# Splitting slabs 36 to 39 of the input projection and moving the recurrence's phase products to VectorE

## The reference

```python
h = _rmsnorm(x, p['norm_mix_w'])
a_v, a_g, b_u, c_z, c_xbc, c_dt = jnp.split(h @ p['w_in'], IN_SPLITS, axis=-1)
ya, conv_a_buf = _conformer_conv(a_v, a_g, ...)
yb, s5_re, s5_im = _s5(b_u, s5_re, s5_im, ...)
yc, conv_c_buf, ssd_state = _mamba2(c_z, c_xbc, c_dt, ...)
x = x + jnp.concatenate([ya, yb, yc], axis=-1) @ p['w_out']
```

## Time and profile before

| | us |
|---|---|
| median of 3 runs | 1803.45 (1802.83 to 1803.63) |
| the profiled execution | 1805.04 |
| its span, first to last instruction | 1803.3 |
| PE busy in the span | 1784.9 (99%) |
| DVE busy | 1139.3 (63%) |
| ACT busy | 739.2 (41%) |
| POOL busy | 258.9 (14%) |

### The profile page before, as it was taken

How to read it: one execution, slowest core, us unless ns; L and a number is a source line. 1 busy time by engine, 2 the same in 40 slices (tenths; PEclk the granted TensorE clock), 3 DMA queues, 4 the chain that set the end, 5 groups by cost and what they waited for, 6 DMA issues and landing times.

```text
span 1803.3 us, 32857 instructions
## 1 busy us (share of the span) xinstructions
PE 1784.9 (99%) x12594; PEld 1640.2 (91%) x12594; DVE 1139.3 (63%) x1976; ACT 739.2 (41%) x1111; POOL 258.9 (14%) x273
## 2 busy tenths in 40 slices
PE   8999999999999999999999999999999999999998
PEld 7877898777779999866999999999999999999998
DVE  6999888888775564443456556665655566546444
ACT  3100575444453343342245344444433345444444
POOL 1024200133421310000132000000000000003200
PEclk9999999999999999999999999999999999999999
DMA  8333544556667585487555555555555556554552
GB/s 255 106 117 106 198 140 138 176 182 208 196 209 240 164 303 164 153 327 265 154 164 164 164 163 163 163 163 164 164 166 165 165 148 185 166 163 160 167 163 99
DMA packets 158390, 316.49 MB, mean 176 GB/s; under 512 B 16986, under 2 KB 39531, under 8 KB 153492
## 3 DMA queue, kind: packets, MB, share of 16 engines
q1 hardware_dynamic: 153525, 307.73, 54.5%
q10 hardware_dynamic: 4776, 7.56, 1.4%
HBM read 300.78 MB, written 14.89 MB: 175 GB/s over the span
## 4 chain that ended last, share of the span: by engine, by line
PE 93%; DVE 4%; DMA 2%; ACT 1%; issue 0%; ACTq 0%; SPq 0%; DVEq 0%
PE bank L909 22%; PE bank L911 21%; PE bank L910 21%; PE bank L872 20%; PE bank L1467 2%; PE bank L1479 1%; DVE xc L2638 1%; DMA kv<-in_cache_mem_v 1%; DMA xtok<-in_x_prompt 1%; PE bank L1489 1%; PE bank L1278 0%; DMA raw<-in_w_out 0%; DVE raw_lo L2665 0%; PE bank L1097 0%; PE bank L958 0%; PE bank L1312 0%
## 5 line engine op out<-in xcount | busy, mean ns | idle before, releaser
L909 PE MATMUL bank<-hhi,whi 128*128 128x288 f32 x2128 | 631.9, 297 | 0.9 <-DVE wlo L2918 0.9
L910 PE MATMUL bank<-hlo,whi 128*128 128x288 f32 x2128 | 628.5, 295 | 0.0
L911 PE MATMUL bank<-hhi,wlo 128*128 128x288 f32 x2128 | 626.3, 294 | 0.0
L2918 DVE TENSOR_TENSOR wlo<-raw,whi 128x1024 fp32r<-128x1024 f32 (+1 forms) x270 | 329.7, 1222 | 377.7 <-ACT whi L1950 377.1
L1950 ACT ACTIVATE whi<-raw 128x1024 fp32r<-128x1024 f32 (+1 forms) x270 | 283.2, 1049 | 509.8 <-PE bank L911 501.9
L911 PEld LDWEIGHTS bank<-hhi,wlo 128*128 128x128 f32 x2128 | 401.6, 189 | 0.0
L909 PEld LDWEIGHTS bank<-hhi,whi 128*128 128x128 f32 x2128 | 399.3, 188 | 2.3 <-DVE wlo L2918 1.9
L910 PEld LDWEIGHTS bank<-hlo,whi 128*128 128x128 f32 x2128 | 400.2, 188 | 0.1
L872 PE MATMUL bank<-hT,raw 128*128 128x288 f32 x640 | 160.1, 409 | 0.0
L872 PEld LDWEIGHTS bank<-hT,raw 128*128 128x128 f32 x640 | 120.0, 190 | 35.0 <-issue 3.1
L1877 ACT ACTIVATE khi<-raw 128x1024 fp32r<-128x1024 f32 x66 | 69.9, 1059 | 109.5 <-PE bank L872 106.4
(11 more groups left out here) (551 smaller groups left out, 2744.4 us busy)
## 6 DMA issues: line engine op xcount, KB each, us to landing
raw<-in_ffn_w_down SPq DMA_DIRECT2D x86, 512.0 KB, 3.8
raw<-in_ffn_w_gate SPq DMA_DIRECT2D x80, 512.0 KB, 3.7
raw<-in_ffn_w_up SPq DMA_DIRECT2D x80, 512.0 KB, 3.7
raw<-in_w_in SPq DMA_DIRECT2D x64, 512.0 KB, 3.7
raw<-in_xa_wk SPq DMA_DIRECT2D x32, 512.0 KB, 3.9
raw<-in_xa_wv SPq DMA_DIRECT2D x32, 512.0 KB, 4.2
raw<-in_w_out SPq DMA_DIRECT2D x32, 512.0 KB, 3.8
raw<-in_xa_wq SPq DMA_DIRECT2D x32, 512.0 KB, 4.0
```

The costliest lines, as they stand in the source:

```text
L909: pe.matmul(out, lhsT=wh[:, wo:wo + P], rhs=xh, start=first, stop=False)
L910: pe.matmul(out, lhsT=wh[:, wo:wo + P], rhs=xl, start=False, stop=False)
L911: return pe.matmul(out, lhsT=wl[:, wo:wo + P], rhs=xh, start=False, stop=last)
L2918: tt(wlo[:, s % 2, wsl], raw[:, s % 4, wsl], whi[:, s % 2, wsl].bitcast(F32), ALU.subtract)\
```

## The change

1. `SPLIT_AT` becomes 36: slabs 36 to 39 are split too. Group 4 is then half plain (slabs 32 to 35, row tiles 0 to 7) and half split (slabs 36 to 39, row tiles 8 to 15).
2. ACT rounds the activations of tiles 8 to 15 right after `in_evac(3)`, ahead of the first taps, and those of tiles 0 to 7 between the splits; `XHI_AT` gives each tile's place in the new order. The functions `first_tap`, `taps_c` and `gelu` only move in the text, and the four first taps with them.
3. The phase products leave POOL and become `s5_products` on DVE, of the step before, between `tAB` and `gri` of a step.
4. `s5_turn_back(j - 1)` moves from the end of step j to the place between `gri` and the scan.
5. DVE's `in_split` of slabs 36 to 41 is placed inside steps 14 and 15 and behind them.
6. `s5_out` of the last pair comes after slab 40 instead of 39.

```diff
-    "pool_setup": (("bsel", 2), ("s5_prod", 2 * SJ), ("s5_fin", 2), ("conf_sum", 2)),
+    "pool_setup": (("bsel", 2), ("s5_fin", 2), ("conf_sum", 2)),
...
-        SPLIT_AT = 40
+        SPLIT_AT = 36
+        XHI_AT = [k - 8 if k >= 8 else k + 8 for k in range(16)]
+        S5_OUT = (22, 25, 27, 30, 32, 35, 37, 40)
...
-            for j in range(SJ):
-                pool.wait_ge(*at("s5_scanned", j + 1))
-                g_ = gri[:, j % 2, :, :]
-                if j >= 1:
-                    pool.wait_ge(*at("s5_h", 2 * j))
-                pool.tensor_tensor(hAB[:, 0, :, :], g_, tabC[:, j, :].unsqueeze(1).to_broadcast([P, 2, NP]),
-                                   ALU.mult).then_inc(S("s5_prod"), 1)
-                pool.tensor_tensor(hAB[:, 1, :, :], g_, tabS[:, j, :].unsqueeze(1).to_broadcast([P, 2, NP]),
-                                   ALU.mult).then_inc(S("s5_prod"), 1)
...
-                                    pe.wait_ge(*at("x_hi", k + 1))
+                                    pe.wait_ge(*at("x_hi", XHI_AT[k] + 1))
...
-                    if x == S5_IN[pair] + 5:
+                    if x == S5_OUT[pair]:
                         s5_out(pair)
...
-                    wait_used_A(sc_, SPLIT_AT - 8 + k // 2)
+                    wait_used_A(sc_, (24 if k >= 8 else 32) + k // 2)
...
+            x_high(range(8, KT))
+
+            def first_tap(dst, dst_s, src, src_s, w, b, name):
...
+            for t in range(4):
+                sc_.wait_ge(*at("u_done", 2 * t + 2))
+                first_tap(va[:, t, 0:NP], vsplit(va[:, t, NP:T], NB), up[:, t, 0:NP], up_sample(t)[:, :, 0:NL],
+                          col(C_CAW + t), col(C_CAB + t), "tap_a")
...
-            x_high(range(12))
-            in_split(SPLIT_AT)
-            x_high(range(12, 14))
+            in_split(36)
+            x_high(range(4))
+            in_split(37)
+            x_high(range(4, 8))
+            in_split(38)
+            in_split(39)
+            in_split(40)
             in_evac(4)
-            in_split(SPLIT_AT + 1)
-            x_high(range(14, KT))
+            in_split(41)
...
-            for x in range(SPLIT_AT, NA):
+            for x in range(40, NA):
...
+            def s5_products(j):
+
+                v.wait_ge(*at("s5_scanned", j + 1))
+                g_ = gri[:, j % 2, :, :]
+                if j >= 1:
+                    v.wait_ge(*at("s5_h", 2 * j))
+                for i, tab in enumerate((tabC, tabS)):
+                    tt(hAB[:, i, :, :], g_, tab[:, j, :].unsqueeze(1).to_broadcast([P, 2, NP]), ALU.mult)\
+                        .then_inc(S("s5_prod"), 1)
...
             for j in range(SJ):
+                if j == 15:
+                    in_split(38)
                 v.wait_ge(*at("s5_in", j // 2 + 1))
...
+                if j == 14:
+                    in_split(36)
+                if j >= 1:
+                    s5_products(j - 1)
                 v.wait_ge(*at("s5_turned", 2 * j + 2))
                 g_ = gri[:, j % 2, :, :]
                 if j >= 2:
                     v.wait_ge(*at("s5_prod", 2 * (j - 1)))
                 me.step(tt(g_[:, 0, :], tAB[:, 0, 0, :], tAB[:, 1, 1, :], ALU.add))
                 me.step(tt(g_[:, 1, :], tAB[:, 0, 1, :], tAB[:, 1, 0, :], ALU.subtract))
-                me.sync()
+                if j == 15:
+                    in_split(39)
+                gri_done = me.n
+                if j >= 1:
+                    s5_turn_back(j - 1)
+                me.reach(gri_done)
                 mag = sc[:, 14, j:j + 1].to_broadcast([P, NP])
...
                 if 2 <= j < 10:
                     x_low((6 + j,))
-                if j >= 1:
-                    s5_turn_back(j - 1)
+                if j == 14:
+                    in_split(37)
+                if j == 15:
+                    in_split(40)
...
+            s5_products(SJ - 1)
+            in_split(41)
             s5_turn_back(SJ - 1)
...
-            in_split(SPLIT_AT)
-            in_split(SPLIT_AT + 1)
```

More of the change, by code:

```diff
@@ L1768, in _, with x_high, in_split @@
             in_evac(3)
+            def x_high(tiles):
+                for k in tiles:
+                    wait_used_A(sc_, (24 if k >= 8 else 32) + k // 2)
+                    sc_.wait_ge(*at("x_lo", k + 1))
+                    a(xhi[:, k, :], hT[:, k, :], ACT.Copy).then_inc(S("x_hi"), 1)
+            def in_split(x):
+                wait_raw(sc_, x // 4, x % 4)
+                if x >= SPLIT_AT + 2:
+                    wait_used_A(sc_, x - 2)
+                if x == 48:
+                    sc_.wait_ge(*at("s5_prod", 2 * SJ))
+                    sc_.wait_ge(*at("s5_turned", 2 * SJ))
+                a(ihi_slot(x), raw[:, x % 4, :], ACT.Copy).then_inc(S("kw_hi"), 1)
+            x_high(range(8, KT))
             def first_tap(dst, dst_s, src, src_s, w, b, name):
@@ L1790, in gelu @@
                     a(uT[:, t, :], uT[:, t, :], ACT.Gelu_apprx_tanh).then_inc(S("s5_gelu"), 1)
-            def x_high(tiles):
-                for k in tiles:
-                    wait_used_A(sc_, SPLIT_AT - 8 + k // 2)
[L1796 to L1807, removed]
             def mem_square(t):
@@ L1882, in _ @@
                     k_split(0)
-                elif x > SPLIT_AT:
+                elif x > 40:
                     in_split(x + 1)
@@ L2543, in last_state, with in_split @@
                     me.step(v.tensor_copy(fin[:, i, j:j + 1], hri[:, j % 2, i, NP - 1:NP]))
+            def in_split(x):
+                v.wait_ge(*at("kw_hi", x - SPLIT_AT + 1))
+                tt(raw_lo[:, x % 4, :], raw[:, x % 4, :], ihi_slot(x).bitcast(F32), ALU.subtract)\
+                    .then_inc(S("kw_lo"), 1)
             for j in range(SJ):
+                if j == 15:
+                    in_split(38)
                 v.wait_ge(*at("s5_in", j // 2 + 1))
```

## The result

The changed kernel takes 1810.99 us (median; 1810.45 to 1812.35), the kernel before 1804.16 beside it: a ratio of 1.0035, interval 1.0024 to 1.0046, so 4 to 8 us slower. The profiled execution took 1810.94 us, 5.9 more than that of before, and its span 1809.2. The forecast was 1809.4, slower.

A forecast was written before the change was run, and what follows sets the result against it. PE, busy 99% of the span, was taken as the bound. Waits of 1.0 + 5.6 + 1.9 + 0.5 less 3.2 saved gave +5.9 us with roundings, on 1803.45: 1809.4 us, range 1806.0 to 1813.5.

The forecast's parts named there:

- PE's own work: Slabs 36 to 39 on PE: four slabs at 3.2 instead of 4.0 us, 3.2 us less if halves are ready.
- A step on DVE: DVE's recurrence step, tAB to scan: 3.10 us with the products against 3.22 before, so moving them costs nothing.
- The turn-back's new place: Turn-back ahead of the scan holds back DVE's later work; PE waits in s5_in(7), starting at 185.3, +1.0 us.
- Slab 36: Its low half ends a 5.64 us chain begun by s5_out(5), ready at 197.2; PE stands 5.6 us.
- Slab 37: Its low half is ready at 202.3, PE is through slab 36 at 200.4: 1.9 us of waiting.
- My last paragraph: Signs of being wrong included a granted clock below 1.00 from 191 on, said to make the time longer.
- The rival of the clock: Clock falls after PE's wait: slab 36 takes 6.4 us, total 1810.7, or 1813.9 if slab 37 is slow too; chance 0.18.
- if only half of slab 36 is slow, nothing is added: Clause on the falling clock: with just half of slab 36 at the lower rate, the total time stays as forecast.
- the higher time, 1813.9: Total if slabs 36 and 37 both run at the lower clock; called likelier than 1810.7 by the skill's rule.
- Slabs 38 to 41: Halves of 38 to 40 in time, s5_out(7) waits 0.5 us, slab 41 starts at 217.9 against 211.98.
- What follows: From slab 41 on PE is the bound with the same work, so the +5.9 us shift stays to the end.
- That rival: Slab 43 lands late behind the glu_w load queued ahead of it: 1 to 2 us more, 1811; chance 0.06.

The follow-up runs named there:

- experiment 8: Changed kernel with turn-backs, early halves of slabs 36 and 37, and VectorE's last three steps put in order of need; 1802.18 us, ratio 0.9984.
- experiment 6: Kernel before with only the phase products moved to VectorE, no early split, turn-back at the end of its step; 1805.24 us, ratio 1.0002.
- experiment 1: Changed kernel with turn-back(j - 1) put back to the end of step j; 1808.93 us, ratio 1.0021.
- experiment 2: Changed kernel with high halves of slabs 36 and 37 ahead of first taps 2 and 3, low halves ahead of turn-back(12); 1805.22 us, ratio 1.0001.
- experiment 4: Changed kernel with twenty filler matmuls on ones between s5_out(5) and slab 36, keeping PE at work; 1810.78 us, ratio 1.0029.
- experiment 10: experiment 8 with s5_y(1) behind low half 36, glu_w loaded behind slab 43, third tap of x = 40 behind low half 42; 1801.32 us, ratio 0.9980.
- experiment 5: Kernel before with the four slabs split as in the change, products left on GpSimd, turn-back at the end of its step; 1808.0 us, ratio 1.0019.
- experiment 9: experiment 8 with the products left on GpSimd and low half 41 ahead of turn-back(15); 1805.65 us, ratio 1.0007.

## Why the prediction was right

**PE's own work.** 4 x 0.8 less: right. In experiment 8 slabs 36 to 37, 38 to 39 and 39 to 40 start 3.26, 3.27 and 3.20 us apart.

**A step on DVE.** "Moving the products costs DVE nothing": right. From `tAB` to the turn-back a step takes 3.07 us (166.95 to 170.02) for 3.10, and experiment 6 finds no loss. The products are 0.68 long and start 0.60 apart, `gri` takes 0.42. The Trainium skill (VectorE: DVE Perf Modes, The DRAIN you can't avoid) has the next one start when the pipe of the last is empty; these rows, with no wait between the two, again don't show it, and the same section says that an instruction which nothing holds starts earlier, which I had passed over.

**The turn-back's new place.** Right in mechanism: s5_in(7) came at 185.11 (+0.78, forecast +1.0), behind a wait of 1.30 us for 0.38, with DVE at work without a stop from turn-back(8) at 164.62 to `tAB` of step 13; undoing it in experiment 1 leaves 0.49 of the 1.30.

**Slab 36.** Right: 197.12 for 197.2, a stand of 5.69 for 5.6. Experiments 1 and 2 cut the chain in two places, and 2.4 us of the stand and all of it went.

**Slab 37.** Here a step was off. I had 1.9 us of waiting with the clock held; there was none, and slab 36 took 2.1 us longer in its place. My last paragraph was wrong in naming a clock below 1.00 as what "would make the time longer". The rival of the clock came true in its mechanism, not in its price: I had slab 36 at the lower level throughout, 6.4 us, and 1.3 us lost behind the 1.9; it took 5.27, with 18 of its 24 matmuls slow, as the clock was back before its end. The forecast's own clause ("if only half of slab 36 is slow, nothing is added") comes near what happened: with three quarters slow, 0.2 to 0.3 us was added, by experiment 4. That slab 37 still started as forecast, 202.39 for 202.3, is a small piece of luck: its low half was there 0.3 us sooner than in my sum, and slab 36 ended that much later. The time alone couldn't tell the forecast's 5.9 us from the rival's 7.2, which both lie within 4.3 to 8.3; the rows do. The Trainium skill (TensorE: Matmul & The Clock Gate, Why this matters for your kernels) warned of the lower rate behind idle gaps: the rows agree, at 0.50 from 196 to 200. I had read from it that the higher time, 1813.9, was the likelier of the two; slab 37 ran at 1.00, so it was not.

**Slabs 38 to 41.** Right: no wait ahead of 38, 39 and 40, 0.41 at s5_out(7) for 0.5, slab 41 at 218.08 for 217.9.

**What follows.** "I carry the shift to the end": right, +6.1 at slab 41, +6.2 at 307 us, +5.9 in the profiled time. `glu_w` was issued at 213.85 (forecast 213.4) and slab 43 was not late for it. That rival showed only where PE was earlier: in experiment 8 slab 43 came 0.4 us late behind `glu_w` (ACT waited 2.85 us for a load of `raw` ahead of its high half, until 213.81), in experiment 10 no more.

The absolute time lies 1.6 us over the forecast; 0.7 of that is the kernel before, which took 1804.16 beside it and not 1803.45. One slip in my range: its high end, 1813.5, was to take in the clock at its worst, which I had put at 1813.9.

## What to carry to other kernels

Where an in-order engine both waits for the bound engine and feeds it, write down for each instruction who wants it next and place the ones that wait longest behind those that are wanted soonest: here the same work was 6 us slower or 3 us faster by its order alone. A buffer's release (turn-back(12) waiting for s5_out(5)) is a start line for everything queued behind it, so nothing that PE needs right after may stand there. Check a repaired stretch by one landmark behind it, read against one ahead of it, and by a second further on: a shift that stays there is the time, as far as one execution tells.

## What the runs showed of the hardware

The granted clock went to 0.50 after PE had stood 5.69, 3.44 and 3.27 us: in the changed kernel while PE still stood (0.69 in the window 194 to 196), in experiments 5 and 1 only after slab 36 had begun, some 0.4 and 1.1 us into it. Each time the first split slab was slow (5.27, 4.97 and 5.09 us for 3.2), and the clock was back at 1.00 before slab 37 began (by 202 us in the changed kernel). After 1.29 or 1.30 us it fell in two profiles and stayed in three others, two of the five being of the same kernel, so a wait of that length has no fixed price.

VectorE and GpSimd hold each other up, and either may pay: in experiment 5 a low half of 1.2 us took 2.22 beside a product begun 0.15 us before it, in experiment 9 a product of 1.3 us took 2.18 beside a low half begun 0.16 us before it, which kept 1.20, and the next product took 3.05 while VectorE's low half and `gri` beside it kept 1.21 and 0.42. The Trainium skill (SBUF — State Buffer, SBUF: two separate sides) says that of a VectorE instruction with two inputs in SBUF and a GpSimd one, whichever starts first holds the ports they share to its end and the other stands. The trace agrees in the first two cases (product from 200.31, low half from 200.46; low half from 197.37, product from 197.53); in the third the two began within 0.01 us of each other, so it can't tell.
